# Norms of a two-layer decoder kernel summed in the stage in front, and new places for the PEER row fetches, dots and transfers

## The reference, cut to what matters

```python
def rms_norm(x, g):
    return x * lax.rsqrt(jnp.mean(x * x, -1, keepdims=True) + EPS) * g

x = attention_layer(x)          # rms_norm(x) @ w_in -> two attention mixers -> x + mixed @ w_out
x = peer_layer(x)
x = sgu_layer(x)                # rms_norm(x) @ w_in -> gelu, spatial gate -> x + y @ w_out
x = peer_layer(x)

def block(xb):                  # in peer_layer, xb = rms_norm(x): 512 tokens x 1024
    q = (xb @ w_query).reshape(-1, 8, 2, 128)
    sc = einsum('thpc,hpkc->thpk', q, sub_keys)      # 128 keys per half
    s1, i1 = top_k(sc[:, :, 0], 16); s2, i2 = top_k(sc[:, :, 1], 16)
    top, ci = top_k(s1[..., :, None] + s2[..., None, :], 16)   # over 256 candidates
    idx = e1 * 128 + e2; g = softmax(top)
    hid = gelu(einsum('td,thkd->thk', xb, expert_down[idx]))
    return einsum('thk,thkd->td', g * hid, expert_up[idx])
```

## Time and profile before

| | |
|---|---|
| median of 3 runs | 3475.59 us |
| lowest, highest | 3459.72, 3480.33 us |
| the profiled execution | 3480.13 us |
| its span on the core | 3478.0 us |
| TensorE busy | 3361.5 us, 97% |
| mean granted clock | 0.964 of 2.4 GHz |
| moved | 808 MB, 232 GB/s mean |

### The profile page before, as it was taken

How to read it: one execution, slowest core, us unless ns; L and a number is a source line. 1 busy time by engine, 2 the same in 40 slices (tenths; PEclk the granted TensorE clock), 3 DMA queues, 4 the chain that set the end, 5 groups by cost and what they waited for, 6 DMA issues and landing times.

```text
span 3478.0 us, 47895 instructions
## 1 busy us (share of the span) xinstructions
PE 3361.5 (97%) x18808; PEld 3050.2 (88%) x18808; DVE 1818.9 (52%) x3788; ACT 1391.9 (40%) x2516; POOL 1853.0 (53%) x1071
## 2 busy tenths in 40 slices
PE   7998899999999899999999998999999999999999
PEld 6755789999999898899988887999999999889998
DVE  4525218995886444444422311699587744444443
ACT  3334223336786333333333322333477733333332
POOL 3400436776677545555544553477767773555553
PEclk9956899999999999999989998999999999999999
DMA  2200124667999888888732222366699998888884
GB/s 106 97 13 1 67 85 163 223 201 269 385 383 394 318 296 320 309 325 318 282 109 97 85 83 81 121 209 199 217 359 383 387 359 304 319 309 318 324 309 165
DMA packets 234302, 808.21 MB, mean 232 GB/s; under 512 B 21088, under 2 KB 70240, under 8 KB 225376
## 3 DMA queue, kind: packets, MB, share of 16 engines
q1 hardware_dynamic: 160352, 536.69, 43.4%
q0 software_dynamic: 73728, 268.47, 20.0%
HBM read 702.32 MB, written 102.76 MB: 231 GB/s over the span
## 4 chain that ended last, share of the span: by engine, by line
PE 84%; DMA 6%; ACT 4%; POOL 3%; DVE 2%; issue 2%; SPq 0%; DVEq 0%; ACTq 0%
PE banks L233 23%; PE banks L234 22%; PE banks L235 22%; PE banks L956 3%; PE banks L920 2%; DMA arena<-down,side 2%; ACT arena L783 2%; POOL weights_lo L213 2%; PE banks L491 2%; PE banks L480 1%; PE banks L248 1%; PE banks L249 1%; PE banks L250 1%; PE banks L280 1%; ACT weights_hi L207 1%
## 5 line engine op out<-in xcount | busy, mean ns | idle before, releaser
L213 POOL TENSOR_TENSOR weights_lo<-raw_ring,weights_hi 128x1024 fp32r<-128x1024 f32 x498 | 1273.0, 2558 | 1121.8 <-ACT weights_hi L207 1120.3
L233 PE MATMUL banks<-operand_hi,weights_hi 128*128 128x384 f32 (+1 forms) x4800 | 1676.5, 349 | 29.0 <-POOL weights_lo L213 14.7
L234 PE MATMUL banks<-operand_lo,weights_hi 128*128 128x384 f32 (+1 forms) x4800 | 1650.1, 344 | 0.0
L235 PE MATMUL banks<-operand_hi,weights_lo 128*128 128x384 f32 (+1 forms) x4800 | 1649.7, 344 | 0.0
L233 PEld LDWEIGHTS banks<-operand_hi,weights_hi 128*128 128x128 f32 x4800 | 906.9, 189 | 118.9 <-issue 73.3
L234 PEld LDWEIGHTS banks<-operand_lo,weights_hi 128*128 128x128 f32 x4800 | 906.9, 189 | 29.3 <-issue 3.6
L235 PEld LDWEIGHTS banks<-operand_hi,weights_lo 128*128 128x128 f32 x4800 | 906.0, 189 | 28.3
L207 ACT CAST weights_hi<-raw_ring 128x1024 fp32r<-128x1024 f32 x624 | 652.9, 1047 | 676.9 <-PE banks L235 580.0
L1121 DVE TENSOR_TENSOR residual<-residual,banks 128x384 f32<-128x384 f32 x256 | 141.9, 554 | 654.8 <-PE banks L235 645.3
L812 ACT ACTIVATE arena<-banks 128x384 f32<-128x384 f32 x256 | 126.0, 492 | 523.3 <-PE banks L235 472.4
L783 ACT ACTIVATE arena<-operand_hi,side 128x128 f32<-128x128 f32 x768 | 235.4, 393 | 51.3 <-DVE operand_hi L1085 46.6
(11 more groups left out here) (175 smaller groups left out, 2798.0 us busy)
## 6 DMA issues: line engine op xcount, KB each, us to landing
raw_ring<-weight_tiles SPq DMA_DIRECT2D x624, 512.0 KB
hid_scratch<-arena SPq DMA_DIRECT2D x64, 768.0 KB
gate_scratch<-arena SPq DMA_DIRECT2D x24, 2048.0 KB
arena<-hid_scratch SPq DMA_DIRECT2D x32, 1536.0 KB
arena<-gate_scratch SPq DMA_DIRECT2D x32, 1536.0 KB
arena<-up,side POOLq DMA_INDIRECT x146
residual<-x_t SPq DMA_DIRECT2D x2, 1024.0 KB, 6.7
arena<-key_t SPq DMA_DIRECT2D x2, 1024.0 KB, 5.1
```

The lines of the kernel that those rows point to most:

```text
L213: eng.tensor_tensor(wl[:, b, :], raw[:, n % RING, :], wh[:, b, :].bitcast(F32), ALU.subtract).then_inc(done, 1)
L233: pe.matmul(out, w_hi, x_hi[:, c, :], start=start and c == 0, stop=False)
L234: pe.matmul(out, w_hi, x_lo[:, c, :], start=False, stop=False)
L235: last = pe.matmul(out, w_lo, x_hi[:, c, :], start=False, stop=stop and c == DC - 1)
```

## The change

It has four parts, for all four norms and both PEER layers.

- **Norms.** Squares of chunks 0 to 6 are made by ScalarE and added up by POOL in one buffer during the last tiles of the stage in front; only chunk 7 remains behind the last residual add. TensorE sums the two buffers. Diagonal blocks are counted and spread singly. Scaled chunks have a ring of four. Even low parts are POOL's, odd ones VectorE's. The first tile (`normed_step`) waits chunk by chunk. The PEER norm's transposes are replaced by 16 matmuls behind tile 1, from high and low part. At the start the masks are loaded behind the first four tiles.
- **Fetches and dots.** 42 dots, evenly, at 17 places of each routed block; 54 over the units; 6 before and 6 behind the first gate slices; two in front of each of the first ten up tiles. Fetches k >= 6 stand one tile behind the tile of dot k - 6.
- **Order.** Units begin at tile 73 (turn at 70). hid group 0 is loaded at down tile 123, gate group 0 at 125, gate group 1 behind hid group 1. Quads begin at up tile 18, 3.1 tiles apart (12 and 3.6 before).
- **End of the up stage.** The quads' sum is turned at up tile 117 and added at 119.

```diff
-        nrm = arena[:, 13312:14336].rearrange("p (b t) -> p b t", b=2)
-        diagonal = arena[:, 14336:14848]
+        diagonal = arena[:, 13312:13824]
+        nrm = arena[:, 13824:15872].rearrange("p (b t) -> p b t", b=NORM_RING)
+        sq_sum = arena[:, 15872:16384]
...
+        def normed_step(pe, n, out, s):
+
+            b = n % WRING
+            wait_lo(pe, n)
+            for c in range(DC):
+                w_hi, w_lo = wh[:, b, c * P:(c + 1) * P], wl[:, b, c * P:(c + 1) * P]
+                pe.wait_ge(s.hi, s.was["hi"] + c + 1)
+                pe.matmul(out, w_hi, oph[:, 0, c, :], start=c == 0, stop=False)
+                pe.matmul(out, w_lo, oph[:, 0, c, :], start=False, stop=False)
+                wait_norm_lo(pe, s, c)
+                last = pe.matmul(out, w_hi, opl[:, 0, c, :], start=False, stop=c == DC - 1)
+            last.then_inc(tiles_done, 1)
...
-        def norm_act(act, s, ready, between=lambda: None):
-            for c in range(DC):
-                ready(act, c)
-                if c >= 2:
-                    act.wait_ge(s.summed, s.was["summed"] + c - 1)
-                act.activation(sq[:, c % 2, :], xt[:, c, :], ACT.Square).then_inc(s.squared, 1)
-            between()
+        def wait_norm_lo(eng, s, c):
+
+            if c % 2 == 0:
+                eng.wait_ge(s.lo_even, s.was["lo_even"] + c // 2 + 1)
+            else:
+                eng.wait_ge(s.lo_odd, s.was["lo_odd"] + c // 2 + 1)
+
+        def norm_square(act, s, c):
+            if c >= 3:
+                act.wait_ge(s.summed, s.was["summed"] + c - 2)
+            act.activation(sq[:, c % 2, :] if c else sq_sum, xt[:, c, :], ACT.Square).then_inc(s.squared, 1)
+
+        def norm_hi(act, s):
             act.wait_ge(s.mean, s.was["mean"] + 1)
             act.activation(root, root, ACT.Sqrt).then_inc(s.root, 1)
             for c in range(DC):
                 act.wait_ge(s.scaled, s.was["scaled"] + c + 1)
-                act.copy(oph[:, 0, c, :], nrm[:, c % 2, :]).then_inc(s.hi, 1)
-
-        def norm_pe(pe, s, x_rows=False):
-            for c in range(DC):
-                pe.wait_ge(s.squared, s.was["squared"] + c + 1)
-                for tt in range(TT):
-
-                    last = pe.matmul(ps[:, 7, tt:tt + 1], sq[:, c % 2, tt * P:(tt + 1) * P], ones[:, 0:1],
-                                     start=c == 0 and tt == 0, stop=c == DC - 1, skip_group_check=True)
-                last.then_inc(s.summed, 1)
-            pe.wait_ge(s.diagonal, s.was["diagonal"] + 1)
-            pe.matmul(ps[:, 7, :], ones, diagonal, start=True, stop=True).then_inc(s.spread, 1)
-            if x_rows:
-                for c in range(DC):
-                    pe.wait_ge(s.scaled, s.was["scaled"] + c + 1)
-                    pe.transpose(ps[:, 5 + c // 4, c % 4 * P:(c % 4 + 1) * P], nrm[:, c % 2, 0:G], ident).then_inc(s.x_turned, 1)
-
-        def norm_dve(dve, s, col, x_rows=False):
-            dve.wait_ge(s.summed, s.was["summed"] + DC)
+                act.copy(oph[:, 0, c, :], nrm[:, c % NORM_RING, :]).then_inc(s.hi, 1)
+
+        def norm_sum(pool, s, c):
+            pool.wait_ge(s.squared, s.was["squared"] + c + 1)
+            if c >= 2:
+                pool.wait_ge(s.summed, s.was["summed"] + c - 1)
+            pool.tensor_tensor(sq_sum, sq_sum, sq[:, c % 2, :], ALU.add).then_inc(s.summed, 1)
+
+        def norm_total(pe, s):
+            pe.wait_ge(s.summed, s.was["summed"] + DC - 2)
+            for tt in range(TT):
+
+                pe.matmul(ps[:, 7, tt:tt + 1], sq_sum[:, tt * P:(tt + 1) * P], ones[:, 0:1], start=tt == 0, stop=False, skip_group_check=True)
+            pe.wait_ge(s.squared, s.was["squared"] + DC)
+            for tt in range(TT):
+                last = pe.matmul(ps[:, 7, tt:tt + 1], sq[:, (DC - 1) % 2, tt * P:(tt + 1) * P], ones[:, 0:1],
+                                 start=False, stop=True, skip_group_check=True)
+            last.then_inc(s.totalled, 1)
+
+        def norm_spread(pe, s):
+            for tt in range(TT):
+                pe.wait_ge(s.diagonal, s.was["diagonal"] + tt + 1)
+                last = pe.matmul(ps[:, 7, tt * P:(tt + 1) * P], ones, diagonal[:, tt * P:(tt + 1) * P], start=True, stop=True)
+            last.then_inc(s.spread, 1)
+
+        def norm_dve(dve, s, col):
+            dve.wait_ge(s.totalled, s.was["totalled"] + 1)
             dve.tensor_scalar(root, ps[:, 7, 0:TT], 1.0 / D, EPS, ALU.mult, ALU.add).then_inc(s.mean, 1)
             dve.wait_ge(s.root, s.was["root"] + 1)
             dve.reciprocal(root, root).then_inc(s.inverse, 1)
             dve.wait_ge(s.inverse, s.was["inverse"] + 1)
-            spread_diagonals(dve, diagonal, root, s.diagonal)
+            for tt in range(TT):
+                dve.tensor_scalar(diagonal[:, tt * P:(tt + 1) * P], ident, root[:, tt:tt + 1], None, ALU.mult).then_inc(s.diagonal, 1)
             dve.wait_ge(s.spread, s.was["spread"] + 1)
+
+            def odd_lo(c):
+                dve.wait_ge(s.hi, s.was["hi"] + c + 1)
+                dve.tensor_tensor(opl[:, 0, c, :], nrm[:, c % NORM_RING, :], oph[:, 0, c, :].bitcast(F32), ALU.subtract).then_inc(s.lo_odd, 1)
+
             for c in range(DC):
-                if c >= 2:
-                    dve.wait_ge(s.lo, s.was["lo"] + c - 1)
-                    if x_rows:
-                        dve.wait_ge(s.x_turned, s.was["x_turned"] + c - 1)
-                dve.scalar_tensor_tensor(out=nrm[:, c % 2, :], in0=xt[:, c, :], scalar=gain[:, col + c:col + c + 1], in1=ps[:, 7, :],
+                if c >= NORM_RING:
+                    wait_norm_lo(dve, s, c - NORM_RING)
+                dve.scalar_tensor_tensor(out=nrm[:, c % NORM_RING, :], in0=xt[:, c, :], scalar=gain[:, col + c:col + c + 1], in1=ps[:, 7, :],
                                          op0=ALU.mult, op1=ALU.mult).then_inc(s.scaled, 1)
+                if c and c % 2 == 0:
+                    odd_lo(c - 1)
+            odd_lo(DC - 1)
 
         def norm_pool(pool, s):
-            for c in range(DC):
+            for c in range(0, DC, 2):
                 pool.wait_ge(s.hi, s.was["hi"] + c + 1)
-                pool.tensor_tensor(opl[:, 0, c, :], nrm[:, c % 2, :], oph[:, 0, c, :].bitcast(F32), ALU.subtract).then_inc(s.lo, 1)
+                pool.tensor_tensor(opl[:, 0, c, :], nrm[:, c % NORM_RING, :], oph[:, 0, c, :].bitcast(F32), ALU.subtract).then_inc(s.lo_even, 1)
...
+                if n == RING - 1:
+                    sp.dma_start(mask, masks).then_inc(masks_loaded, 16)
...
             for s in range(ATT_OUT):
                 ahead_hi(act, N_ATT + ATT_QK + ATT_V + s)
+                if s:
+                    act.wait_ge(att_added, s)
+                    norm_square(act, pn[0], s - 1)
...
         def attention_pool(pool):
+            for c in range(1, DC - 1):
+                norm_sum(pool, an, c)
             for n in range(AHEAD):
                 split_lo(pool, n, lo_pool)
             norm_pool(pool, an)
...
-        UNIT_FROM = 70
+        UNIT_FROM = 73
         UNIT_TILE = [UNIT_FROM + u * 7 // 8 for u in range(UNITS)]
         TURN_TILE = UNIT_FROM - 3
-        EARLY_DOTS = 12
+        ROUTE_DOTS, UNIT_DOTS, TAIL_DOTS = 42, 54, 12
         QUADS = G // 4
         DENSE = (0, 1, 7)
-        QUAD_TILE = [12 + q * 36 // 10 for q in range(QUADS)]
+        QUAD_TILE = [18 + q * 31 // 10 for q in range(QUADS)]
+        W_TILE = 11
...
-        GATHER_DOWN_AT = [17 + k for k in range(DOWN_RING)]
-        GATHER_DOWN_AT += [36 + (k - 6) % 4 + (k - 6) // 4 * 16 for k in range(6, 6 + EARLY_DOTS)]
-        GATHER_DOWN_AT += [UNIT_TILE[min((k - 18) // 2, UNITS - 1)] + 1 + max(0, (k - 18) // 2 - UNITS + 1)
-                           for k in range(6 + EARLY_DOTS, P)]
-        GATHER_UP_AT = [PDOWN - 3 + j for j in range(UP_RING)]
+        def dot_tile(k):
+
+            if k < ROUTE_DOTS:
+                return 19 + k * 51 // ROUTE_DOTS
+            k -= ROUTE_DOTS
+            if k < UNIT_DOTS:
+                return UNIT_TILE[k * UNITS // UNIT_DOTS]
+            k -= UNIT_DOTS
+            if k < TAIL_DOTS:
+                return UNIT_TILE[-1] + 1 + k
+            return PDOWN + (k - TAIL_DOTS) // 2
+
+        GATHER_DOWN_AT = [17 + k // 2 if k < DOWN_RING else dot_tile(k - DOWN_RING) + 1 for k in range(P)]
+        UP_ORDER = [6] + [(P - DOWN_RING + i) % DOWN_RING for i in range(DOWN_RING)]
+        GATHER_UP_AT = [PDOWN - 4] + [dot_tile(P - DOWN_RING + i) + 1 for i in range(DOWN_RING)]
         GATHER_UP_AT += [PDOWN + QUAD_TILE[(j - UP_RING) // 4] + 1 + (j - UP_RING) % 4 // 2 for j in range(UP_RING, P)]
...
-                if h == PDOWN - 7:
+                if h == UNIT_TILE[-1] + 9:
                     load_hid(0)
+                if h == UNIT_TILE[-1] + 11:
                     for half in range(2):
                         sp.wait_ge(s.gate_stored[half], was["gate_stored"] + 16 * (GATE_BLOCKS // 2))
                     load_gate(0)
-                    load_gate(1)
...
```

(46 more changed lines are left out.)

116 lines of the change are left out of this document (73 added, 43 removed).

## The result

The changed kernel takes **3440.2 us** (median of 6 runs, 3434.89 to 3442.96) against 3463.54 us for the kernel before (median of 6, 3450.47 to 3480.33) measured beside it: ratio 0.992, 95% interval 0.9891 to 0.9948. Forecast were 3408 us. So the change is real, but 23 us instead of 68; the time lies at the upper end of the stated range (3366 to 3444), outside the forecast's own (3388 to 3432), and the gain of 0.8% is within the 1% to which the forecast gave a chance of 0.10. The profiled execution of the new kernel is its fastest, 3434.89 us, span 3433.1.

A forecast was written before the change was run, and what follows sets the result against it. TensorE, busy 97%, bounds the kernel, so only its holes can be won: norms 50, end 5, down stage 13, together 68 us off 3480.1, and 4.5 for the median, give 3408 us. Range 3366 to 3444, the forecast's own 3388 to 3432.

The forecast's parts named there:

- Norms: All four norms: less work behind the last residual add was to win 50 us together, bounds 42 and 57.
- The turn: Down tile 70 of each PEER layer: TensorE stands waiting for VectorE's routing, costing 6 us a layer.
- New end: Layer 0's routing: start, bare work, 42 dots of 1.15 us and 14.7 us of fetch wait end at 820.9.
- 171.9 bare: Old routing of the other three blocks: 192.85 us without 12 dots of 1.15 us and a 7.2 us fetch wait.
- by the numbers the dot is past before the fetch's turn: First ten up tiles: POOL's fetch was not expected to wait for the dot six before it.
- rival C: Turn: VectorE's lateness costs TensorE 1:1; 1.3 us wait per routing dot makes 52 us a layer, 3512 us; chance 0.03.
- Units: Unit stretch of the down stage: 3 us a layer lost to two-unit tiles waiting on ScalarE; DMA at 318 GB/s.
- Tail: Behind the units, per layer: 2 us left of the former 13, 15 into the up stage, 5 in its first ten tiles.
- Down to up: Start of up stage: VectorE's group 1 slice waits for hid and gate loads, 15 us a layer, bounds 7 and 20.
- B: Down stage returns nothing or costs: turn 12 us late, first up tiles at upper ends, middle -20, 3441 us; chance 0.10.
- Rival D: Clock stays at 1.2 GHz through each first tile: three norms lose 2.4 us each, 3415 us, inside the forecast.

## Why the forecast was wrong

**Norms: the sum right, two details wrong.** These are the rows that answer to the earlier trace rows. Last residual add, squares 6 and 7 and the ones-matmuls, mean, diagonals, first scaling, first tile:

```profile
381.18 0.69 DVE L666 TENSOR_TENSOR residual<-residual,banks 128x512 f32<-128x512 f32 x1 [4.75 <-PE banks L251]
...
382.58 1.05 PE L310 MATMUL banks<-constants,arena 128*128 128x1 f32 x8 [0.66 <-ACT arena L288]
383.67 0.16 DVE L322 TENSOR_SCALAR small<-banks 128x4 f32<-128x4 f32 x1 [1.81 <-PE banks L310]
...
384.31 0.87 DVE L327 TENSOR_SCALAR arena<-constants,small 128x128 f32<-128x128 f32 x4
...
386.77 2.07 DVE L337 SCALAR_TENSOR_TENSOR arena<-residual,gain_columns,banks 128x512 f32<-128x512 f32 x3 [1.58 <-PE banks L317]
...
388.25 2.97 POOL L346 TENSOR_TENSOR operand_lo<-arena,operand_hi 128x512 fp32r<-128x512 f32 x2 [7.74 <-ACT operand_hi L295]
388.31 0.76 PE L235 MATMUL banks<-operand_hi,weights_hi 128*128 128x512 f32 x1 [1.58 <-ACT operand_hi L295]
...
388.86 1.21 DVE L332 TENSOR_TENSOR operand_lo<-arena,operand_hi 128x512 fp32r<-128x512 f32 x1
...
391.46 0.63 PE L235 MATMUL banks<-operand_hi,weights_hi 128*128 128x512 f32 x1
...
392.74 0.63 PE L235 MATMUL banks<-operand_hi,weights_hi 128*128 128x512 f32 x1
...
396.70 0.39 PE L249 MATMUL banks<-operand_hi,weights_hi 128*128 128x512 f32 x1
```

Mean at +2.49 (forecast +2.35), first scaling at +5.59 (+4.48), first tile through at +15.5 (between +14.5 and +16.7), second at 402.14, +21.0 (+21.6), x rows 3.57 us (3.5). The two details: the spread was priced at 2.4 GHz. The granted clock is 0.50 there, that is 1.2 GHz, after TensorE had only ones-matmuls behind its last tile, and its eight instructions take 2.08 us; in the spatial and the second PEER norm at 1.00 they take 1.16 and the first scaling comes 2.18 and 2.19 us behind the mean as forecast (2.13), here 3.10. And the first tile is not paced by low parts. Its chunks from the second on are 1.28 us apart (391.46, 392.74), which is TensorE at 0.63 us a matmul, its 1.2 GHz level, and fall to 0.68 when it is back at 2.4 GHz at 393.98. The stretches, spread, first chunks, last four, columns as above:

```profile
384.60:386.70 2.10, 2.04 (x8) 1.78 (x8) 0.59 (x3) 0.00 (x0) 0.00 (x0) 0.50 1.01 423
388.30:393.90 5.60, 5.51 (x12) 3.93 (x13) 5.52 (x8) 3.44 (x6) 4.17 (x3) 0.50 0.05 20
394.00:396.70 2.70, 2.70 (x13) 2.24 (x12) 1.50 (x3) 1.66 (x3) 1.51 (x2) 1.00 0.00 0
```

The low parts end 9.4 us behind the first scaling (9.6 forecast), 0.3 us before the tile's last matmul starts: low parts and clock set nearly the same pace, so the sum held, in part by luck. That POOL and VectorE take turns shows in line 332, which takes 1.21 us when it starts beside POOL's first subtraction and ends 0.55 us behind it, and 0.69 alone.

**The turn: the step that failed.** The text said "New end: 586.04 + 171.9 + 42 x 1.15 + 14.7". Start of block 1 (60.06 us behind the first down tile), dots and the wait for the first row (14.9) came as written. The 171.9 did not: from the start of block 1 to the end of the last dot the new kernel takes 801.7 - 556.4 = 245.3 us, 10.4 more than 171.9 + 48.3 + 14.7, and the subtraction behind it 1.1 us more than forecast; VectorE is through 11.5 us later than in the sum. The instruction groups of VectorE in that window show 9 of the 10.4. First the kernel before (lines 1053 and 1054), then the new one (1148 and 1150), the same 12 instructions:

```profile
L1054 DVE TENSOR_TENSOR operand_lo<-operand_lo,side 128x2048 fp32r<-128x2048 f32 x6 | 26.2, 4374 | 0.2
L1053 DVE TENSOR_TENSOR operand_lo<-side,constants 128x2048 fp32r<-128x2048 f32 x6 | 13.8, 2293 | 0.2
```

```profile
L1148 DVE TENSOR_TENSOR operand_lo<-side,constants 128x2048 fp32r<-128x2048 f32 x6 | 27.5, 4588 | 0.1
...
L1150 DVE TENSOR_TENSOR operand_lo<-operand_lo,side 128x2048 fp32r<-128x2048 f32 x6 | 21.6, 3608 | 0.1
```

Alone such an instruction takes 2.29 us; it takes up to 5.67 when POOL's subtractions and fetches fall beside it. Before, the second of each pair was lengthened, always to 4.37 or 4.38, and the first never; now nine of the twelve are, three of them beyond 4.6: 49.1 us instead of 40.0. "171.9 bare" was not bare, it held the meetings of one particular order of VectorE's and POOL's work, and the change gives both engines another order. In the run with the first dot later the two lines take 21.4 + 21.7, 6.0 less; the shorter waits for rows give 7.6, line 1117 and smaller ones take 2.7 more, and that is the 11 us that VectorE gained. What makes the meetings more frequent (the extra points for dots between the two instructions, or the denser fetches) was not separated.

**POOL's queue: the sentence "by the numbers the dot is past before the fetch's turn" fell with it.** The fetch of row k stands in POOL's queue at the tile at which dot k - 6 is due by plan. VectorE is behind its plan from the first wait on, up to 15 us, so twelve fetches stand for dots (28.3 us), the next split stands behind them, and TensorE has 9.7 us of holes before the turn, with the clock at 0.99. I had priced TensorE's wait at the turn only, 6 us. It arrived there late already and waited 1.2; the rest of the 15.6 are small gaps and the slower clock behind the holes. The loss is what VectorE's lateness is (310.3 + 0.7 against 295.5), as rival C's rule says (1:1).

**Units: right.** 3 us forecast, 2.5 measured, 310 GB/s (318 forecast), one dot wait of 1.3 us. What I missed is how much room was left: 84 dots instead of 54 cost 1 to 2 us more.

**Tail: mechanism right, too small by 4 to 7 us a layer** (22 forecast, 25.9 and 29.4 measured). The chain behind the down stage:

```profile
1100.83 14.99 DMA arena<-gate_scratch
1115.84 3.84 DVE arena L1199 x8
1119.68 1.13 DVE pair L1082
...
1121.10 0.95 POOL pair L930
1122.07 2.38 POOL weights_lo L216
1124.58 0.66 PE banks L249
...
1139.33 5.47 DMA hid_scratch<-arena
...
1145.29 13.35 DMA arena<-gate_scratch
1158.67 0.57 DVE arena L1199
```

The second part is the hole of "Down to up": 11.8 us of waiting for the split behind group 1's first slice, with load_gate(1) 13.35 us in flight. The first part was not in the sum: group 0's gates take 15 us to come, eight slices and a dot stand on VectorE, a fetch on POOL for that dot, a split behind the fetch: 3.2 us of hole. Of the 25.9 us 19 are holes and the rest is the clock, 0.93 over 142 us against 1.00. load_gate(1) early took 4 us a layer out, and 16 dots fewer in the up stage, with it early in both, another 12 and 14.

**The sum.** The down stage is 29.7 us off (13 forecast, -16.7 measured); the attention's chance difference gave 4.4 and the norms 2 the other way; the profile comes to 3434.9 instead of 3412. I then took off 4.5 us for the median against the profiled execution, which holds for the kernel before; the new kernel's median lies 5 above its profile. Together 32 us. Of the 29.7 us the turn has 19 (15.6 + 15.3 against 2 x 6) and the tail 11 (25.9 + 29.4 against 2 x 22). So some 10 of the 32 us are the choice of executions, not the schedule.

**The rivals.** B, "the down stage returns nothing or costs", at 3441 with a chance of 0.10, is nearest to what happened, 3440 us and -17 for its -20, with VectorE 15.5 us late for the turn where it names 12. Rival C's 52 us are a slip: 42 dots of 1.3 us are 54.6. Rival D's 1.2 GHz held for about half of the first PEER layer's first tile (388.3 to 393.9). B should have had more: each piece of the VectorE schedule was "near its limit", and they hang on the same engine, so they can fail together.

## What to carry to other kernels

When dots, splits or fetches are spread over another engine's work, price the receiving engine by its instructions at their durations in company, and give wide two-input SBUF instructions beside a busy POOL nearly twice their bare time (here 49.1 us for 27.5). In a plan that ties a queue (fetch of k + 6) to another engine's progress (dot k), the first wait counts: start the consumer when its first input can be there, not at the first free place. And of work with a hard tail behind it, put as much into the stretch in front as its engines have slack for (here 84 dots, with 25 us of VectorE's slack left), little behind: 16 dots moved from the up stage to the units took 12 and 14 us out of the tail and cost 2 beside the units in layer 0, none in layer 1.

## What the runs showed of the hardware that I had not expected

A full DMA share is not yet a loss. From the first to the last unit it is 1.00 with 84 dots (370 GB/s) and with 96 (379 GB/s), and the stretch loses 4 and 18 us. As long as VectorE has slack, the wait for late rows stays there.

POOL's fetch instruction is lengthened beside VectorE too, not only subtractions. Line 930 over the new kernel's execution, minimum, median, maximum ns, and one case in layer 0:

```profile
L930 POOL DMA_INDIRECT arena<-down,side x126: 933/952/3028, 577.6 to 2858.4; - x126
```

```profile
709.69 5.67 DVE L1148 TENSOR_TENSOR operand_lo<-side,constants 128x2048 fp32r<-128x2048 f32 x1
...
713.36 2.82 POOL L930 DMA_INDIRECT pair<-down,side  x1 [0.16 <-issue]
```

Eleven of the 42 fetches of layer 0's routing take 2.82 to 3.03 us instead of 0.95, 22 in the two layers. Each of the 22 ends 0.82 to 0.84 us behind the end of a two-input VectorE instruction of 128x2048, wherever it began: here 716.18 against 715.36. In the kernel before, none of the 256 takes over 1.09 us. So the fetch is held until VectorE's instruction is through. Two fetches that began within 0.05 us of the start of such an instruction ran in 0.95 us. The Trainium skill, "SBUF — State Buffer", section "SBUF: two separate sides", says that while VectorE runs an instruction in a 2-port performance mode, POOL is locked out of the shared port pair and can't write the descriptors of a DMA from its own queue. The trace agrees on the blocking, 0.95 us grown to 3.03, for instructions with two SBUF inputs, which that sentence does not name. I had used that page's rule for the norm's subtractions and not for the 42 fetches and 12 wide instructions of the routing, where it cost 9 us a layer on VectorE alone.
